# Two-layer mixer trunk: the second norm of layer 1, the routing and the scatter of the rows as one phase

## What is computed

```python
h = modulate(rms_norm(x, norm2_g[l]), sh2, sc2)

def moe_swiglu(h, router_w, router_b, w1, w3, w2):
    t = h.reshape(B * S, D)
    probs = jax.nn.softmax((t @ router_w + router_b).astype(jnp.float32), axis=-1)
    top_p, top_i = lax.top_k(probs, TOP_K)
    top_p = top_p / jnp.sum(top_p, axis=-1, keepdims=True)
    flat_e = top_i.reshape(-1)
    order = jnp.argsort(flat_e)
    tok = order // TOP_K
    sizes = jnp.bincount(flat_e, length=N_EXPERTS).astype(jnp.int32)
    xs = t[tok]
    hid = jax.nn.silu(lax.ragged_dot(xs, w1, sizes)) * lax.ragged_dot(xs, w3, sizes)
    y = lax.ragged_dot(hid, w2, sizes) * top_p.reshape(-1)[order][:, None].astype(h.dtype)
    out = jnp.zeros((n_tok, D), h.dtype).at[tok].add(y)
```

## Time and profile before

| | us |
|---|---|
| median of 3 runs | 5873.48 (5871.64 to 5876.23) |
| the profiled execution | 5873.49 |
| its span, first to last instruction | 5871.70 |
| TensorE (PE) busy with matmuls | 5379.5 (92%) |
| VectorE (DVE) busy | 2402.2 (41%) |
| GpSimd (POOL) busy | 1828.6 (31%) |
| ScalarE (ACT) busy | 1816.8 (31%) |

### The profile page before, as it was taken

One profiled execution on the slowest core, in us unless ns is written; L12 is line 12 of the kernel. 1 busy time (PEld: TensorE's weight loads), 2 busy tenths in 40 slices (PEclk: granted clock), 3 DMA queues, 4 the chain that ended last, 5 costly groups with the idle time before them and its releaser, 6 DMA issues. The chain is left out here.

```text
span 5871.7 us, 72382 instructions
## 1 busy us (share of the span) xinstructions
PE 5379.5 (92%) x29832; PEld 4516.4 (77%) x29833; DVE 2402.2 (41%) x2154; ACT 1816.8 (31%) x1515; POOL 1828.6 (31%) x498
## 2 busy tenths in 40 slices
PE   7997799989999899779986699999999999999995
PEld 4675577768888667557765699899889898898985
DVE  6346333323624533621122243343373336743356
ACT  3112111132122211311112234333363335643344
POOL 1410111134444231011110425243265236641543
PEclk8998899999999999889996899999999999999997
DMA  4210222323635521011120756555595558975568
GB/s 165 76 61 15 72 81 80 99 79 106 196 97 157 155 61 58 22 36 45 45 89 16 240 182 200 192 192 181 185 329 194 179 194 273 335 234 179 193 229 293
DMA packets 810335, 853.64 MB, mean 145 GB/s; under 512 B 19155, under 2 KB 731987, under 8 KB 809811
## 3 DMA queue, kind: packets, MB, share of 16 engines
q1 hardware_dynamic: 802178, 820.19, 43.4%
q0 software_dynamic: 4608, 16.78, 0.8%
q10 hardware_dynamic: 3408, 14.68, 0.6%
HBM read 793.90 MB, written 57.67 MB: 145 GB/s over the span
## 5 line engine op out<-in xcount | busy, mean ns | idle before, releaser
L2094 POOL TENSOR_TENSOR e_w_lo<-e_raw,e_w_hi 128x2048 fp32r<-128x2048 f32 x170 | 1073.7, 6326 | 1477.8 <-ACT e_w_hi L2032 1477.8
L257 PE MATMUL banks<-e_x_hi,e_w_hi 128*128 128x256 f32 x3584 | 1019.6, 284 | 34.9 <-issue 23.8
L258 PE MATMUL banks<-e_x_lo,e_w_hi 128*128 128x256 f32 x3584 | 1018.5, 284 | 0.0
L259 PE MATMUL banks<-e_x_hi,e_w_lo 128*128 128x256 f32 x3584 | 1018.4, 284 | 0.0
L251 POOL TENSOR_TENSOR w_lo<-w_raw,w_hi 128x1024 fp32r<-128x1024 f32 (+1 forms) x216 | 514.5, 2382 | 1601.7 <-ACT w_hi L246 1601.7
L2032 ACT ACTIVATE e_w_hi<-e_raw 128x2048 fp32r<-128x2048 f32 x340 | 648.4, 1912 | 541.3 <-PE banks L259 530.3
L257 PEld LDWEIGHTS banks<-e_x_hi,e_w_hi 128*128 128x128 f32 x3584 | 692.7, 193 | 38.3 <-issue 25.9
L258 PEld LDWEIGHTS banks<-e_x_lo,e_w_hi 128*128 128x128 f32 x3584 | 692.7, 193 | 0.0
L259 PEld LDWEIGHTS banks<-e_x_hi,e_w_lo 128*128 128x128 f32 x3584 | 692.5, 193 | 0.0
L257 PE MATMUL banks<-h_hi,w_hi 128*128 128x512 f32 x1408 | 565.5, 402 | 32.6 <-DVE h_lo L779 22.8
L270 PE MATMUL banks<-h_hi,w_hi 128*128 128x512 f32 x1280 | 527.3, 412 | 74.2 <-POOL w_lo L251 57.7
(11 more groups left out here) (298 smaller groups left out, 8312.9 us busy)
## 6 DMA issues: line engine op xcount, KB each, us to landing
e_raw<-in_moe_w_dram SPq DMA_DIRECT2D x510, 1024.0 KB, 5.0
w_raw<-in_ffn_w_dram SPq DMA_DIRECT2D x120, 512.0 KB, 3.9
w_raw<-in_w_in_dram SPq DMA_DIRECT2D x108, 512.0 KB, 4.0
f_ada_raw<-in_ada_w_dram SPq DMA_DIRECT2D x48, 512.0 KB, 5.0
g_ada_raw<-in_ada_w_dram SPq DMA_DIRECT2D x32, 512.0 KB, 3.9
e_io<-row_scratch SPq DMA_DIRECT2D x13, 1024.0 KB, 7.0
x_scratch<-x_res SPq DMA_DIRECT2D x24, 512.0 KB, 3.1
row_scratch<-stage SPq DMA_DIRECT2D x24, 512.0 KB, 2.6
```

Source lines behind the costliest of these rows:

```text
L257: pe.matmul(out, wh, rh, start=first, stop=False)
L258: pe.matmul(out, wh, rl, start=False, stop=False)
L259: return pe.matmul(out, wl, rh, start=False, stop=last)
L2094: eng.tensor_tensor(flat(w_lo[u]), flat(raw[n % RING]), flat(w_hi[u]).bitcast(F32), ALU.subtract).then_inc(lo_sem[u % 2], 1)
```

## The change

The three phases `norm_phase`, `route_phase` and `scatter_phase` become one, `route_phase`, with 25 semaphores. Norm, squares and sums stand in it as they were. What is different:

- SP loads the router's weights and the bias (now 8 values on 8 partitions) at the start of the joint phase, and stores the zeros there too; POOL clears the buffer, in place of VectorE.
- The logits are computed transposed: the 8 columns of the router's weights rest in TensorE, 512 tokens of `h_f` move, 16 matmuls, each channel tile as soon as it is written. ScalarE adds the bias on its way out of PSUM (`r_logit_t`, 8 partitions by 1024 tokens), and 8 small transposes bring the logits back to tokens on partitions.
- TensorE turns token tiles 0 and 1 before those small transposes and tiles 2 to 7 after them. ScalarE copies two tiles out, runs Exp, and copies the other six.
- The eight maxima, and then the eight index searches, follow each other without a wait between them. `r_both` comes before the weights of the pair.
- The ranks take two matmuls over all 64 columns of `r_both`: ones (the counts of each token tile) and the triangular matrix (the rank within the tile). VectorE adds the counts up over the tiles in eight chained steps (`r_before`), and adds them to the ranks.
- POOL waits for the slots and the row copies, not for the table, and scatters while VectorE computes the table and SP takes it through DRAM.

```diff
-    rb = m.place("router_b_sb", [P, NE], F32, m.route + 256)
+    rb = m.place("router_b_sb", [NE, 1], F32, m.route + 256)
+    zero = m.place("zeros", [P, 2, D], F32, m.R + 72 * KB)
...
+    before = m.place("r_before", [P, ST + 1, NE], F32, big + 3200)
...
             sp.dma_start(rw[:, :, :], a.router_w[e].rearrange("(k p) n -> p k n", p=P)).then_inc(s.w_in, 16)
-            sp.dma_start(rb[:, :], a.router_b[e].partition_broadcast(P)).then_inc(s.w_in, 16)
+            sp.dma_start(rb[:, :], a.router_b[e].rearrange("(n o) -> n o", o=1)).then_inc(s.w_in, 16)
+            sp.wait_ge(s.zeroed, 1)
+            sp.dma_start(a.rows[SLOTS:SLOTS + ITEM, :].rearrange("(t p) n -> p t n", p=P), zero[:, :, :]).then_inc(s.filled, 16)
+            sp.wait_ge(s.filled, 16)
             sp.wait_ge(s.tab, 1)
             sp.dma_start(a.items, tab[0:MAX_ITEMS + 1, :]).then_inc(s.saved, 16)
             sp.wait_ge(s.saved, 16)
             sp.dma_start(m.items[:, :], a.items.rearrange("(o i) c -> o (i c)", o=1)).then_inc(s.back, 16)
             sp.wait_ge(s.back, 16)
+        @block.gpsimd
+        def _(pool):
+            pool.memset(zero[:, :, :], 0.0).then_inc(s.zeroed, 1)
+            pool.wait_ge(s.h_in, ST)
+            pool.wait_ge(s.slots, 1)
+            for t in range(ST):
+                for q in range(2):
+                    pool.indirect_dma_start(a.rows, bass.IndirectOffsetOnAxis(ap=m.slot[:, t, q:q + 1].bitcast(U32), axis=0),
+                                            m.hrow[:, t, :], None).then_inc(s.scattered, 16)
+            pool.wait_ge(s.scattered, 16 * 2 * ST)
...
         @block.tensor
         def _(pe):
...
             pe.wait_ge(s.w_in, 32)
-            for t in range(ST):
-                for k in range(KT):
-                    last = pe.matmul(m.ps[:, 7, NE * t:NE * t + NE], m.h_f[:, k, P * t:P * t + P], rw[:, k, :],
+            for k in range(KT):
+                pe.wait_ge(s.hi, k + 1)
+                for half in range(NHALF):
+                    last = pe.matmul(m.ps[0:NE, 6 + half, :], rw[:, k, :], m.h_f[:, k, half * HALF:(half + 1) * HALF],
                                      start=(k == 0), stop=(k == KT - 1))
             last.then_inc(s.logits, 1)
-            for t in range(ST):
+            def turn(t):
                 if t >= 2:
                     pe.wait_ge(s.h_in, t - 1)
                 for k in range(KT):
                     last = pe.transpose(m.ps[:, 2 * (t % 2) + k // 4, P * (k % 4):P * (k % 4 + 1)],
                                         m.h_f[:, k, P * t:P * t + P], cst[:, K_ID:K_ID + P])
                 last.then_inc(s.turned, 1)
+            pe.wait_ge(s.root, 1)
+            for t in range(2):
+                turn(t)
+            pe.wait_ge(s.lg_in, 1)
+            for t in range(ST):
+                last = pe.transpose(m.ps[:, 5, NE * t:NE * t + NE], lgt[:, P * t:P * t + P], cst[0:NE, K_ID:K_ID + NE])
+            last.then_inc(s.lg_turned, 1)
+            for t in range(2, ST):
+                turn(t)
             pe.wait_ge(s.hot, 1)
-
-            for t in range(ST):
-                for u in range(t + 1):
-                    w = K_LOW if u == t else K_ONE
-                    last = pe.matmul(m.ps[:, 6, NE * t:NE * t + NE], cst[:, w:w + P], both[:, u, :], start=(u == 0), stop=(u == t))
-            for u in range(ST):
-                last = pe.matmul(m.ps[:, 5, 0:NE], cst[:, K_ONE:K_ONE + P], both[:, u, :], start=(u == 0), stop=(u == ST - 1))
-            last.then_inc(s.ranked, 1)
+            both2 = both[:, :, :].rearrange("p t e -> p (t e)")
+            pe.matmul(m.ps[:, 4, 0:ST * NE], cst[:, K_ONE:K_ONE + P], both2, start=True, stop=True)
+            pe.matmul(m.ps[:, 4, ST * NE:2 * ST * NE], cst[:, K_LOW:K_LOW + P], both2, start=True, stop=True).then_inc(s.ranked, 1)
...
         @block.scalar
         def _(act):
...
+            act.wait_ge(s.logits, 1)
+            act.activation(lgt[:, :], m.ps[0:NE, 6:8, :].rearrange("p a n -> p (a n)"), ACT.Identity, bias=rb[:, 0:1]).then_inc(s.lg_in, 1)
+            def h_row(t):
                 act.wait_ge(s.turned, t + 1)
                 act.activation(m.hrow[:, t, :], m.ps[:, 2 * (t % 2):2 * (t % 2) + 2, :].rearrange("p a n -> p (a n)"), ACT.Copy).then_inc(s.h_in, 1)
+            for t in range(2):
+                h_row(t)
             act.wait_ge(s.shifted, 1)
             act.activation(pr[:, :, :], lg[:, :, :], ACT.Exp).then_inc(s.exped, 1)
+            for t in range(2, ST):
+                h_row(t)
...
-            dve.wait_ge(s.logits, 1)
-            dve.wait_ge(s.w_in, 32)
-            chain(dve.tensor_tensor(lg[:, :, :], m.ps[:, 7, 0:ST * NE].rearrange("p (t e) -> p t e", e=NE), row(rb), ALU.add))
...
+            chain(dve.memset(before[:, 0, :], 0.0))
+            dve.wait_ge(s.lg_turned, 1)
+            chain(dve.tensor_copy(lg[:, :, :], m.ps[:, 5, 0:ST * NE].rearrange("p (t e) -> p t e", e=NE)))
...
             for t in range(ST):
-                chain(dve.max(top[:, t, :], pr[:, t, :]))
-                chain(dve.max_index(idx[:, t, :], top[:, t, :], pr[:, t, :]))
+                last = dve.max(top[:, t, :], pr[:, t, :])
+            chain(last)
+            for t in range(ST):
+                last = dve.max_index(idx[:, t, :], top[:, t, :], pr[:, t, :])
+            chain(last)
             chain(dve.tensor_copy(idx_f[:, :, :], idx[:, :, :]))
+            experts = row(cst[:, K_EXP:K_EXP + NE])
+            for q, one in enumerate((one0, one1)):
+                chain(dve.tensor_tensor(one[:, :, :], idx_f[:, :, q:q + 1].broadcast_to([P, ST, NE]), experts, ALU.is_equal))
+            dve.tensor_tensor(both[:, :, :], one0[:, :, :], one1[:, :, :], ALU.add).then_inc(s.hot, 1)
             chain(dve.tensor_tensor(tw[:, :], top[:, :, 0], top[:, :, 1], ALU.add))
             chain(dve.reciprocal(tw[:, :], tw[:, :]))
-            experts = cst[:, K_EXP:K_EXP + NE].rearrange("p (o e) -> p o e", o=1).broadcast_to([P, ST, NE])
-            for q, one in enumerate((one0, one1)):
-                chain(dve.tensor_tensor(m.top_w[:, :, q], top[:, :, q], tw[:, :], ALU.mult))
-                chain(dve.tensor_tensor(one[:, :, :], idx_f[:, :, q:q + 1].broadcast_to([P, ST, NE]), experts, ALU.is_equal))
-            dve.tensor_tensor(both[:, :, :], one0[:, :, :], one1[:, :, :], ALU.add).then_inc(s.hot, 1)
+            for q in range(2):
+                dve.tensor_tensor(m.top_w[:, :, q], top[:, :, q], tw[:, :], ALU.mult)
             dve.wait_ge(s.ranked, 1)
-            chain(dve.tensor_copy(cnt[:, :], m.ps[:, 5, 0:NE]))
+            for t in range(ST):
+                chain(dve.tensor_tensor(before[:, t + 1, :], before[:, t, :], m.ps[:, 4, NE * t:NE * t + NE], ALU.add))
+            cnt_v = before[:, ST, :]
...
-            prefix(off, cnt)
-            chain(dve.tensor_tensor(rank[:, :, :], m.ps[:, 6, 0:ST * NE].rearrange("p (t e) -> p t e", e=NE), row(off), ALU.add))
+            prefix(off, cnt_v)
+            chain(dve.tensor_tensor(rank[:, :, :], m.ps[:, 4, ST * NE:2 * ST * NE].rearrange("p (t e) -> p t e", e=NE), before[:, 0:ST, :], ALU.add))
+            chain(dve.tensor_tensor(rank[:, :, :], rank[:, :, :], row(off[:, :]), ALU.add))
...
-            chain(dve.tensor_copy(m.slot[:, :, :], slot_f[:, :, :]))
-
-            chain(dve.tensor_scalar(nch[:, :], cnt[:, :], 0.0, None, ALU.is_gt))
+            dve.tensor_copy(m.slot[:, :, :], slot_f[:, :, :]).then_inc(s.slots, 1)
+            chain(dve.tensor_scalar(nch[:, :], cnt_v, 0.0, None, ALU.is_gt))
...
-def scatter_phase(nc, m, a):
...
@@ -2394,9 +2397,7 @@
                 dense_phase(nc, m, a, l)
             else:
                 moe_memory(m)
-                norm_phase(nc, m, l)
                 route_phase(nc, m, a, l)
-                scatter_phase(nc, m, a)
                 expert_phase(nc, m, a, l)
                 combine_phase(nc, m, a, l)
```

More of the change, by code:

```diff
@@ L1770, in route_phase @@
     mx, sm, inv, tw = (m.place(n, [P, ST], F32, big + 2560 + 32 * i) for i, n in enumerate(("r_mx", "r_sm", "r_inv", "r_tw")))
[L1771 to L1772 removed]
+    off, nch, end, beg, c0, c1, hot, val = (m.place(n, [P, NE], F32, big + 2688 + 32 * i) for i, n in enumerate(
+        ("r_off", "r_nch", "r_end", "r_beg", "r_c0", "r_c1", "r_hot", "r_val")))
     tab_f = m.place("r_tabf", [P, 4], F32, big + 3072)
@@ L1775, in route_phase @@
     slot_f = m.place("r_slotf", [P, ST, 2], F32, big + 3136)
+    before = m.place("r_before", [P, ST + 1, NE], F32, big + 3200)
     e = l // 2
-    with phase(nc, "w_in", "turned", "h_in", "logits", "shifted", "exped", "hot", "ranked", "step", "tab", "saved", "back") as (block, s):
+    with phase(nc, "squared", "summed", "root", "inv", "scaled", "hi",
+               "w_in", "zeroed", "filled", "turned", "h_in", "logits", "lg_in", "lg_turned", "shifted", "exped", "hot", "ranked", "step",
+               "slots", "scattered", "tab", "saved", "back") as (block, s):
         @block.sync
@@ L1814, in _ @@
```

(16 more changed lines are left out.)

87 lines of the change are left out of this document (26 added, 61 removed).

## The result

The changed kernel takes **5814.5 us** (median of 4 runs, 5809.6 to 5816.7), the kernel before 5873.35 in 4 runs beside it: ratio 0.9898, 95% interval 0.9881 to 0.9915. Forecast were 5811.1 and a range of 5804 to 5827. Timed again in another session (after_again) it takes 5812.5 (4 runs, 5808.97 to 5814.52) against 5874.4 (7 runs): 0.9893, 0.9877 to 0.991. The two medians lie 3.4 and 1.4 above the forecast; the four times of the first spread by 7.1.

A forecast was written before the change was run, and what follows sets the result against it. Engines taking turns between the output projection and the experts were taken as the bound, TensorE busy 75.9 of 169.5 us. 23.7 + 9.3 + 18.2 - 1.7 + 10.7 + 2.2 = 62.4 off 5873.49 gave 5811.1, range 5804 to 5827.

The forecast's parts named there:

- Logits: TensorE's router logits: start at the first `h_f` row, 32 records in 16.0 us; gain 23.7, bounds 13.7 to 27.3.
- The first rival: TensorE's clock stays at 1.2 GHz through the logits, which end 11.3 later; time 5826.6; chance 0.10.
- Logits to hot: From the logits' end through transposes, Exp and VectorE's chain to `r_both`, with TensorE's turning meeting it within 0.2; gain 9.3.
- Ranks: Two rank matmuls, four records, 0.7 us, replace 88 short records; waiting for counts falls from 19.03 to 0.9; gain 18.2.
- VectorE after the ranks: From counts to slots: one copy goes, eight chained sums and one addition come; 4.8 instead of 3.14; loss 1.7.
- Slots to scatter: POOL no longer waits for the table, its DRAM transfers and a phase's end, 10.9 before; gain 10.7.
- Scatter: First indirect issue to experts' request: 2.5 gained without the zeros' store, 0.3 lost to table operations; net 2.2 gained.
- Priced at nothing: Zeros' memset and store and router loads, covered by the norm; the table's transfers, covered by the scatter: no cost.
- The Trainium skill's rule on transposes: Says the full clock does not engage for transposes; would make the sum some 4 us smaller; the forecast followed the trace.
- Rivals 2 and 3: 2: table operations delay the scatter, 5816.3, chance 0.07. 3: scatter waits for row copies, 5816.7 at 10 us slip, 0.03.
- Rival 4: Slower than before: TensorE's "issue" stops ahead of the experts' first matmuls become more frequent; 5885 at 20 more; chance 0.01.
- The range and the signs: Own range 5804 to 5818; signs included `r_before` under 1.5 us after `r_both`, first indirect DMA within 0.5 of slots.

The follow-up runs named there:

- ranks_old: The changed kernel with the 44 short rank matmuls back and VectorE copying the counts instead of adding them in eight steps; 5883.68 us.
- pad_42: The changed kernel with 42 idle matmuls of 8 columns (+168 TensorE instructions) added behind the two rank matmuls; 5870.22 us, against 5871.46 for the kernel before.

## Why the prediction was right

The likeliest case happened: the stretch gave 61.45 where the sum said 62.4, and the experts' stretch kept its length within 1.4. By its steps:

- **Logits** (23.7): 23.05. They began some 0.15 later and took 16.54 instead of 16.0, mostly since the clock rose 5.3 us in and not 4.6. The first rival, no rise at all, fell.
- **Logits to hot** (9.3): 10.93, from 19.16 to 8.23. Exp's end came 4.57 behind the logits, forecast 4.6. From there to `r_both` VectorE needed 3.66 instead of 5.2: I had taken off 0.03 for each chained step that goes, but the eight maxima and eight searches now take 1.87 (3162.63 to 3164.50) where a pair of them stood 0.48 from the next before, 3.8 for all. The forecast let TensorE and VectorE arrive together; TensorE turned rows until about 3166.9, 1.4 behind `r_both`, and alone set the start of the ranks.
- **Ranks** (18.2): 17.07, since the 1.96 from `r_both` to the counts hold this waiting for TensorE; from the start of the two matmuls it is 0.60, forecast 0.7. The two errors nearly cancel. ranks_old gives back 13.9: its 17.30 from `r_both` (3169.14) to the counts against 1.96, less some 1.5 for the eight sums that VectorE is spared. Of the 17.30, 1.36 are this waiting too; from their start the old ranks need 15.9 against 19.0 before, so the clock left up by the new logits is worth 3.0 to them.
- **VectorE after the ranks** (-1.7): -1.63; 4.77 from counts to slots, 4.8 forecast.
- **Slots to scatter** (10.7): 9.96. From slots to the first issue 0.94 pass, not 0.2: a waiting POOL takes longer to start than I allowed.
- **Scatter** (2.2): 2.07, from 29.83 to 27.76. The 0.3 lost to the table was not there: beside it the issues take 0.96 and 0.95, as before. That leaves 2.07 where I gave the zeros 2.5, but no run stores them where the kernel before did, so what they are worth alone is not shown.
- **Priced at nothing:** memset and store of the zeros lay in the norm (1.80 from 3112.86, store at 3114.69), the table's two transfers were issued at 3177.66 and 3179.97, 21 us before the request. Their cover held.
- **The Trainium skill's rule on transposes**, "TensorE: Matmul & The Clock Gate", Part 4, again disagrees with the trace: the granted clock was 1.00 from 3157.2 to 3167.4, where nearly all work is transposes, and 16 took 1.96 to 2.01.
- **Rivals 2 and 3** fell: the table did not hold the scatter up (priced at 5.2), and the last row copy had ended at 3168.1, 4.1 ahead of the slots.
- **Rival 4** did not happen, but of all that was written it was weighed most wrongly. A shift of the program ahead does cost the experts' loop 57 us at +168 instructions and 77 at +216, where I had priced 74. The stops grow longer, though, and not more frequent: there are eight in the kernel before, in after_again and in pad_42. I argued against it that the experts' instructions are unchanged; their place was not, and three of the four places tried from +168 to +256 lose the gain. What I could not see in one trace is where a loop stands within 256 instructions. The kernel before and the changed one both stand on the good side, which is luck and no part of the forecast's reasoning; 0.01 was too low a chance for it.
- **The range and the signs.** The terms of my own range add up to 5805 to 5820 and not to 5804 to 5818. Two of the signs that I named did not come: `r_before` starts 1.96 behind `r_both`, not under 1.5, and POOL's first indirect DMA 0.94 behind the slots, not within 0.5.

## What to carry to other kernels

Where engines take turns, cost the change as a list of time stamps and forecast each: two errors of 1 us that cancelled show only there. Let the small operand rest and the long one move, put a chain of small matmuls into one where the algebra allows, and put what nobody waits for (a table, row copies) behind what somebody does. And before a change of instruction count ahead of a loop is judged by its time, shift the loop by padding and look at the stops for "issue" and the instruction queue's transfers: a gain of 60 us can vanish, or appear, by that alone.

## What was not expected of the hardware

- The same loop takes 2604 to 2607, 2662 to 2664 or 2683 us, by the number of TensorE instructions ahead of it (+0 and +256, +168 and +176, +216), with 103 to 105 or 152 instruction transfers; eight stops grow from 2.0 to 8.5 us each to 7.8 to 14.2.
- TensorE's granted clock fell from 1.00 to 0.50 during unbroken matmuls of 8 columns (ranks_old, 1.00 from 3168 to 3172, 0.50 from 3176); it was 1.00 from 3157.2 to 3167.4 in the changed kernel, where nearly all work is transposes of 128 columns.
- POOL's first indirect issue after a wait takes 1.15 and starts 0.94 behind the slots; the following ones take 0.95. Beside fp32 copies on VectorE they take 1.15, beside two-input additions 0.95.
- The zeros' store of 1 MB, put 0.85 us ahead of the first issue of a scatter that keeps the DMA engines 97% busy, lengthens the stretch by 0.7 only.
